# Shared-expert weight tiles lent to the routed-expert stream; shared gate loaded and multiplied later

## The reference, cut to what matters

```python
def moe_ffn(h, router_w, router_bias, w_gate, w_up, w_down, ws_gate, ws_up, ws_down):
    t = h.reshape(-1, d)
    scores = jax.nn.sigmoid((t @ router_w).astype(jnp.float32))
    ...
    _, top_idx = lax.top_k(jnp.where(exp_mask, biased, -jnp.inf), TOP_K)
    ...
    def expert_block(args):
        tb, gb = args
        a = jax.nn.silu(jnp.einsum('td,edf->tef', tb, w_gate)) * jnp.einsum('td,edf->tef', tb, w_up)
        return jnp.einsum('tef,efd->td', a * gb[..., None], w_down)
    ...
    shared = (jax.nn.silu(t @ ws_gate) * (t @ ws_up)) @ ws_down
```

## Time and profile before

| | |
|---|---|
| median of 3 runs | 642.48 us (641.2 to 643.05) |
| the profiled execution | 643.33 us, of which the span is 641.7 us |
| PE busy | 581.4 us, 91% of the span |
| DMA traffic | 252.55 MB, mean 394 GB/s |
| mean granted PE clock | 0.974 of full |
| chain that ended last | PE 70%, DMA 20%, SP's queue 4% |

### The profile page before, as it was taken

How to read it: one execution, slowest core, us unless ns; L and a number is a source line. 1 busy time by engine, 2 the same in 40 slices (tenths; PEclk the granted TensorE clock), 3 DMA queues, 4 the chain that set the end, 5 groups by cost and what they waited for, 6 DMA issues and landing times.

```text
span 641.7 us, 11143 instructions
## 1 busy us (share of the span) xinstructions
PE 581.4 (91%) x4568; PEld 404.7 (63%) x4568; DVE 211.7 (33%) x479; ACT 167.6 (26%) x308; POOL 32.7 (5%) x78
## 2 busy tenths in 40 slices
PE   0789999999999999989999999596999999998776
PEld 0478777688867576756675757363667676765343
DVE  0287777787832222011212221020121212122104
ACT  3164726672622121111221212010212121212010
POOL 1240210010200000000000000000000000000002
PEclk9989999999999999999999999797999999999779
DMA  8999599989998999999999999999999999999995
GB/s 330 386 332 400 205 367 379 411 314 398 420 388 367 393 422 416 421 422 419 421 421 421 420 421 421 421 421 421 420 421 421 419 422 422 420 420 421 422 386 172
DMA packets 50662, 252.55 MB, mean 394 GB/s; under 512 B 5912, under 2 KB 11680, under 8 KB 26288
## 3 DMA queue, kind: packets, MB, share of 16 engines
q1 hardware_dynamic: 47808, 245.85, 94.5%
q0 software_dynamic: 1840, 4.21, 2.1%
q10 hardware_dynamic: 960, 1.74, 0.7%
HBM read 250.06 MB, written 1.72 MB: 392 GB/s over the span
## 4 chain that ended last, share of the span: by engine, by line
PE 70%; DMA 20%; SPq 4%; ACT 2%; DVE 2%; issue 1%; POOL 0%; POOLq 0%; DVEq 0%; ACTq 0%
PE bank L1286 24%; PE bank L1361 12%; DMA ring<-in_w_up 8%; PE bank L1257 7%; PE bank L1303 7%; DMA ring<-in_w_gate 4%; DMA ring<-in_w_in 4%; SPq L572 3%; PE bank L856 2%; DMA ring<-in_w_mod 2%; PE bank L898 2%; PE bank L906 2%; PE bank L902 2%; DMA ccol<-in_c 2%; PE bank L1019 1%; PE bank L1220 1%
## 5 line engine op out<-in xcount | busy, mean ns | idle before, releaser
L1286 PE MATMUL bank<-ring,xe 128*64 128x256 f32 (+1 forms) x1520 | 176.6, 401 | 10.5 <-DMA ring<-in_w_up 8.7
L1286 PEld LDWEIGHTS bank<-ring,xe 128*64 128x64 f32 (+1 forms) x1520 | 111.0, 132 | 50.4 <-issue 24.8
L1361 PE MATMUL bank<-ring,actT 128*64 128x512 f32 (+1 forms) x384 | 86.6, 627 | 6.8 <-DMA ring<-in_w_down 5.2
L2334 DVE TENSOR_TENSOR act_e<-bank,sil 128x256 f32<-128x256 f32 x26 | 11.0, 424 | 187.9 <-ACT sil L1749 187.9
L2348 DVE SCALAR_TENSOR_TENSOR ylo<-bank,gslot,yhi 128x512 fp32r<-128x512 f32 x50 | 37.5, 751 | 83.9 <-ACT yhi L1762 83.9
L1762 ACT ACTIVATE yhi<-bank,gslot 128x512 fp32r<-128x512 f32 x50 | 34.4, 687 | 116.5 <-PE bank L1361 116.5
L1749 ACT ACTIVATE sil<-bank 128x256 f32<-128x256 f32 x26 | 10.0, 385 | 192.1 <-PE bank L1286 192.1
L1257 PE MATMUL bank<-pone,hhi 128*128 128x256 f32 x200 | 50.0, 288 | 0.0
L1361 PEld LDWEIGHTS bank<-ring,actT 128*64 128x64 f32 (+1 forms) x384 | 25.4, 132 | 37.7 <-issue 37.4
L1257 PE MATMUL bank<-pone,hlo 128*128 128x256 f32 x200 | 48.9, 282 | 0.0
L1286 PE MATMUL bank<-rows_tile,xe 128*64 128x256 f32 (+1 forms) x128 | 34.2, 428 | 9.8 <-DMA ring<-in_w_up 6.3
(11 more groups left out here) (388 smaller groups left out, 838.9 us busy)
## 6 DMA issues: line engine op xcount, KB each, us to landing
ring<-in_w_gate SPq DMA_DIRECT2D x49, 1024.0 KB, 25.0
ring<-in_w_down SPq DMA_DIRECT2D x48, 1024.0 KB, 26.3
ring<-in_w_up SPq DMA_DIRECT2D x46, 1024.0 KB, 26.1
ring<-in_w_mod SPq DMA_DIRECT2D x12, 2048.0 KB, 13.9
ring<-in_w_in SPq DMA_DIRECT2D x5, 2048.0 KB, 16.5
gb<-in_w_up SPq DMA_DIRECT2D x5, 1024.0 KB, 23.8
spare<-in_w_gate SPq DMA_DIRECT2D x4, 1024.0 KB, 26.8
ring<-in_w_out SPq DMA_DIRECT2D x2, 2048.0 KB, 18.8
```

The costliest lines, as they stand in the source:

```text
L1286: ins = mm(bank[6][j * w:(j + 1) * w, part * FE:(part + 1) * FE], xe[:, k, slots], weights[:, k, :], start=(k == 0), stop=(k == KD - 1))
L1361: ins = mm(bank[4 + h][j * w:(j + 1) * w, :], actT[:, f, j * w:(j + 1) * w], weights[:, f, 512 * h:512 * h + 512], start=(f == 0), stop=(f ...
```

## The change

The three tiles of `ws` become three more places of the stream (`WS_UP`, `WS_DOWN`, `WS_GATE`). The first fill grows from 16 tiles to 19: g = 18, 16 and 17 are loaded where, and when, the shared gate, up and down were. `rows_tile` takes g = 22 instead of g = 20: it used to follow four refills and now follows three.

The shared gate is loaded just ahead of g = 37, into `WS_GATE`, once g = 18 has been used (in unit 1), and stays. `WS_UP` and `WS_DOWN` go on serving the stream up to unit 8; shared up and down are loaded ahead of g = 107, the last tile of unit 8, once g = 89 and g = 90 have been used.

PE multiplies no shared gate before the counts; it multiplies both halves in unit 2, and ACT applies one Silu to 512 columns instead of two to 256. The bank that held the first half is no longer waited for. The semaphores of the three products are one, and PE waits for each tile's load.

```diff
-SPARE, OVER_GB, OVER_XN, OVER_Y, OVER_ROWS = NTILE, NTILE + 1, NTILE + 2, NTILE + 3, NTILE + 4
-FILL = [0, 1, OVER_Y, 2, 3, 4, 5, 6, 7, 8, 9, 10, OVER_XN, SPARE, OVER_GB, 11]
-ROWS_FREE = len(FILL) + 4
+SPARE, OVER_GB, OVER_XN, OVER_Y, OVER_ROWS, WS_UP, WS_DOWN, WS_GATE = range(NTILE, NTILE + 8)
+FILL = [0, 1, OVER_Y, 2, 3, 4, 5, 6, 7, 8, 9, 10, OVER_XN, SPARE, OVER_GB, 11, WS_UP, WS_DOWN, WS_GATE]
+ROWS_FREE = len(FILL) + 3
+SHARED_UNIT = 8
...
-        while place[taken] == OVER_Y or (kept == OVER_GB and place[taken] in (OVER_GB, OVER_XN)):
+        while (place[taken] == OVER_Y or (kept == OVER_GB and place[taken] in (OVER_GB, OVER_XN)) or
+               place[taken] == WS_GATE or (len(place) >= SHARED_UNIT * NTILE and place[taken] in (WS_UP, WS_DOWN))):
+            if place[taken] in (WS_UP, WS_DOWN, WS_GATE):
+                shared[place[taken]] = (len(place), taken)
             taken += 1
...
-            sp.dma_start(ws[:, 0:EW].rearrange("p (k f) -> p k f", k=KD),
-                         t["ws_gate"][0].rearrange("(k p) f -> p k f", k=KD)).then_inc(wsg_loaded, 16)
-            sp.dma_start(ws[:, EW:2 * EW].rearrange("p (k f) -> p k f", k=KD),
-                         t["ws_up"][0].rearrange("(k p) f -> p k f", k=KD)).then_inc(ws_loaded, 16)
+            load_first(NTILE + 6)
+            load_first(NTILE + 4)
...
-            sp.dma_start(ws[:, 2 * EW:3 * EW], t["ws_down"][0].rearrange("(p j) n -> p (j n)", j=JF)).then_inc(ws_loaded, 16)
+            load_first(NTILE + 5)
...
+            def load_shared(at):
+                for where_, (g, taken) in SHARED.items():
+                    if g == at:
+                        released(taken)
+                        if where_ in (WS_UP, WS_GATE):
+                            source = t["ws_up" if where_ == WS_UP else "ws_gate"][0]
+                            sp.dma_start(tile(where_).rearrange("p (k f) -> p k f", k=KD),
+                                         source.rearrange("(k p) f -> p k f", k=KD)).then_inc(tile_loaded[where_], 16)
+                        else:
+                            sp.dma_start(tile(WS_DOWN),
+                                         t["ws_down"][0].rearrange("(p j) n -> p (j n)", j=JF)).then_inc(tile_loaded[WS_DOWN], 16)
...
                     g = unit * NTILE + i
+                    load_shared(g)
...
-            pe.wait_ge(wsg_loaded, 16)
-            complete("sg0", shared_product(claim("sg0"), 0, (0,)))
...
-                shared_product(bank[7], 0, (1,)).then_inc(sg_filled, 1)
+                pe.wait_ge(tile_loaded[WS_GATE], PLACE.count(WS_GATE) * 16 + 16)
+                shared_product(bank[7], 0).then_inc(shared_filled, 1)
...
-            ps = product(act, "sg0")
-            drain("sg0", A(ssil[:, 0, :], ps[:, 0:NST * P], ACT.Silu))
...
-                A(ssil[:, 1, :], bank[7][:, NST * P:2 * NST * P], ACT.Silu).then_inc(sg_copied, 1)
+                A(ssil[:, :, :], bank[7][:, :].rearrange("p (a b) -> p a b", a=JF), ACT.Silu).then_inc(sg_copied, 1)
```

More of the change, by code:

```diff
@@ L66 @@
 FIRST_STEP = [sum(1 if v in QUAD_UNITS else 2 for v in range(u)) for u in range(UNITS)]
-SPARE, OVER_GB, OVER_XN, OVER_Y, OVER_ROWS = NTILE, NTILE + 1, NTILE + 2, NTILE + 3, NTILE + 4
-FILL = [0, 1, OVER_Y, 2, 3, 4, 5, 6, 7, 8, 9, 10, OVER_XN, SPARE, OVER_GB, 11]
-ROWS_FREE = len(FILL) + 4
+SPARE, OVER_GB, OVER_XN, OVER_Y, OVER_ROWS, WS_UP, WS_DOWN, WS_GATE = range(NTILE, NTILE + 8)
+FILL = [0, 1, OVER_Y, 2, 3, 4, 5, 6, 7, 8, 9, 10, OVER_XN, SPARE, OVER_GB, 11, WS_UP, WS_DOWN, WS_GATE]
+ROWS_FREE = len(FILL) + 3
+SHARED_UNIT = 8
 def place_tiles():
-    place, replaces, free = list(FILL), [None] * len(FILL), []
+    place, replaces, shared = list(FILL), [None] * len(FILL), {}
     taken = 0
@@ L87, in place_tiles @@
     nth = [place[:g + 1].count(p) for g, p in enumerate(place)]
-    return place, replaces, nth
-PLACE, REPLACES, NTH = place_tiles()
+    return place, replaces, nth, shared
+PLACE, REPLACES, NTH, SHARED = place_tiles()
 def build(nc, t, o, overflow_at=CAP):
@@ L125, in build @@
         plan += [("hb0_0", 7, 2), ("hb0_1", 3, 2)] + banks("x2T1:2 x2T3:0 rt1:5") + [("hb1_0", 2, 2), ("hb1_1", 6, 2)]
-        plan += banks("sg0:4 pos:1 counts:5")
+        plan += banks("pos:1 counts:5")
         plan = [(name, b, 2 if name in ("pv0", "pv1", "hm0", "hm1", "xT0", "xT1", "xT2", "xT3") else reads)
@@ L332, in build @@
         qk_loaded, grow_loaded, ml_loaded, cm_loaded = sem("qk_loaded"), sem("grow_loaded"), sem("ml_loaded"), sem("cm_loaded")
-        wsg_loaded, ws_loaded, rt_loaded = sem("wsg_loaded"), sem("ws_loaded"), sem("rt_loaded")
+        rt_loaded = sem("rt_loaded")
         consts, const_masks = sem("consts"), sem("const_masks")
@@ L365, in build @@
         hT_low, hT_high = sem("hT_low"), sem("hT_high")
-        sg_filled, sg_copied = sem("sg_filled"), sem("sg_copied")
+        shared_filled, sg_copied = sem("shared_filled"), sem("sg_copied")
         dve_done, pool_done = sem("dve_done"), sem("pool_done")
         out_done = sem("out_done")
-        tile_loaded = [sem(f"tile_loaded{i}") for i in range(NTILE + 5)]
+        tile_loaded = [sem(f"tile_loaded{i}") for i in range(NTILE + 8)]
         last_columns = [sem(f"last_columns{i}") for i in range(2)]
@@ L380, in build @@
         y_filled, y_hi, y_lo = sem("y_filled"), sem("y_hi"), sem("y_lo")
-        gate_ready, su_filled = sem("gate_ready"), sem("su_filled")
+        gate_ready = sem("gate_ready")
         c_used, all_done, scaled, last_gated = sem("c_used"), sem("all_done"), sem("scaled"), sem("last_gated")
@@ L479, in tile @@
             if i >= NTILE:
-                return (spare[:, :], gb[:, :, :].rearrange("p s d -> p (s d)"), xn[:, 0:EW], over_yhl[:, :], rows_tile[:, :])[i - NTILE]
+                return (spare[:, :], gb[:, :, :].rearrange("p s d -> p (s d)"), xn[:, 0:EW], over_yhl[:, :], rows_tile[:, :],
+                        ws[:, EW:2 * EW], ws[:, 2 * EW:3 * EW], ws[:, 0:EW])[i - NTILE]
             return ring[:, i * EW:(i + 1) * EW]
@@ L1169, in _, with shared_product @@
             turn_back(1)
-            def shared_product(ps, off, parts=range(JF)):
+            def shared_product(ps, off):
                 w = ws[:, off:off + EW].rearrange("p (k f) -> p k f", k=KD)
-                for j in parts:
+                for j in range(JF):
                     for k in range(KD):
@@ L1210, in shared_up @@
             def shared_up():
-                pe.wait_ge(ws_loaded, 32)
-                shared_product(bank[7], EW).then_inc(su_filled, 1)
+                pe.wait_ge(tile_loaded[WS_UP], PLACE.count(WS_UP) * 16 + 16)
+                shared_product(bank[7], EW).then_inc(shared_filled, 1)
             def shared_down():
+                pe.wait_ge(tile_loaded[WS_DOWN], PLACE.count(WS_DOWN) * 16 + 16)
                 wd = ws[:, 2 * EW:].rearrange("p (j n) -> p j n", j=JF)
@@ L1230, in gather_first @@
                 evacuated(pe, "x2T3")
-                evacuated(pe, "sg0")
+                evacuated(pe, "rt0")
                 pe.wait_ge(first_stream, 1)
@@ L1764, in shared_gate @@
             def shared_gate():
-                act.wait_ge(sg_filled, 1)
-                A(ssil[:, 1, :], bank[7][:, NST * P:2 * NST * P], ACT.Silu).then_inc(sg_copied, 1)
+                act.wait_ge(shared_filled, 1)
+                A(ssil[:, :, :], bank[7][:, :].rearrange("p (a b) -> p a b", a=JF), ACT.Silu).then_inc(sg_copied, 1)
             def keep_g2(n, first):
@@ L2391, in shared_act @@
             def shared_act():
-                dve.wait_ge(su_filled, 1)
+                dve.wait_ge(shared_filled, 2)
                 dve.wait_ge(sg_copied, 1)
```

## The result

| | before | changed |
|---|---|---|
| median | 641.79 us (640.78 to 643.05, 6 runs) | 645.32 us (644.59 to 646.97, 6 runs) |
| ratio | | 1.0056, 95% interval 1.0043 to 1.0069 |
| profiled execution | 643.33 us, span 641.7 us | 644.59 us, span 643.0 us |
| mean granted PE clock | 0.974 | 0.963 |

The change made the kernel 3.5 us slower, 0.56%. The forecast was 3.3 us: 645.8 against a median of 642.48. The two profiled executions lie only 1.3 us apart, because the one of the changed kernel was 1.7 us ahead when the routing was done (171.89 us against 173.58). It was 0.7 us ahead at 17 us, in code that the change doesn't touch.

What follows compares the result with a forecast made beforehand. DMA traffic was taken to bound the kernel from 216 us on. Against the profiled 643.33 us, 0 (memory) + 0 (rows tile) + 0.9 (1 KB pieces) + 0 (shared gate) + 2.4 (clock) = 646.6; as median 645.8 us, range 643.0 to 647.2.

Steps and rivals of the forecast that it cites:

- The bound: From 216 us on, DMA traffic at 421 GB/s sets the end; only earlier bytes or a faster rest would help.
- The lent memory at 0: Three routed tiles replace three shared ones in the first fill, adding no bytes by 216 us: 0.
- The rows tile at 0: Loading `rows_tile` earlier gains up to 2.1 us at 192 to 196 us, lost again after 212 us: 0.
- the second hole: Traffic dip to 199 GB/s from 192 to 196 us, costing 2.1 us; forecast to be filled by `rows_tile`.
- the third: Traffic dip to 320 GB/s from 212 to 216 us, costing 1.0 us; forecast to grow by 2.1 us.
- The 1 KB pieces at 0.9 us: Shared gate and up, loaded in the full stretch at 356 GB/s instead of 421, cost 2 x 0.46 us.
- The clock at 2.4 us: PE idle 3.85 us before the counts; its clock halves, delaying the first gate product and whole stream by 2.4 us.
- the open gap: PE's idle time from 169.73 to 173.58 us, before the counts, where the eight matmuls were taken out: 3.85 us.
- No fall: Rival: PE's clock stays at 1.00 after the gap, leaving only 0.9 us: 643.4 us, same by measurement; chance 0.21.

Runs made afterwards that it cites:

- e6_not_lent: Changed kernel with the first fill cut to the old 16 tiles and the `ws` memory empty until the late shared loads: 652.22 us, ratio 1.0145 to the kernel before.
- e9_delay: Kernel before plus eight dense matmuls, result unused, directly ahead of the first gate product: 646.03 us against 641.76, ratio 1.0056.
- e1_fill: Changed kernel with eight matmuls, result unused, put back on PE ahead of the counts: 643.38 us against 642.53 for the kernel before, ratio 1.0013.
- e2_fill_8k: e1_fill with shared gate and up also read as 8 KB rows per partition: 642.49 us, ratio 0.9992 to the kernel before.
- e3_gate_moved: Kernel before with only the shared gate's first half moved from before the counts to unit 2: 644.23 us against 642.53, ratio 1.0028.
- e8_gap_fill: Kernel before plus two matmuls, result unused, between the counts and the gather: 641.66 us against 641.76, ratio 0.9996.
- e10_fill_both: Changed kernel with eight matmuls ahead of the counts and two between counts and gather: 643.06 us against 642.28 for the kernel before, ratio 1.0021.
- e4_rows_early: Kernel before with only `rows_tile` moved to follow three refills instead of four: 642.21 us against 642.53, ratio 0.9995.

## Why the prediction was right

- **The bound.** Right. From 216 us to the end of the stream the traffic is full in both kernels, PE's longer work in unit 2 disappeared in its waits, and `e6_not_lent` and `e9_delay` priced the two things that count before: a place (1.9 to 2.3 us) and PE's time ahead of the first release (about 1 us for 1 us, with an interval of 2.2 to 4.9 us for 3.4).
- **The lent memory at 0.** Right. `e6_not_lent` shows that the value is large but was there before.
- **The rows tile at 0.** Right in its effect, in part wrong in its working. The forecast had the second hole vanish and the third grow by 2.1 us; in the kernel with that edit alone the second shrank by 0.7 us and the third grew by 0.1. The sum took for granted that the few tiles issued there keep the engines at 421; the 381 GB/s say that they didn't, and why stays open. In the changed kernel the second hole kept 1.7 us and the third grew by 0.3. There `rows_tile` came free later than forecast, too: its cast starts at 190.83, 18.9 us after the first count instead of 16.4 (189.98 - 173.58), as much later as PE's first gate product.
- **The 1 KB pieces at 0.9 us.** Right in place and, as far as times can tell, in size: 0.9 us by the medians between `e1_fill` and `e2_fill_8k`. That it is the size of the pieces, and not how far apart they lie, is not shown. The Trainium skill (DMA: Bandwidth & Descriptors, Specifications) has transfers from 512 B on at line rate. These loads in pieces of 1 KB ran below it, at 350 against 423 GB/s.
- **The clock at 2.4 us.** Right. The fall came 4.0 us after PE stopped (168.04 to 172.03), inside the 2.4 to 4.2 us read from the rows, and lasted the 6.8 us read from them; PE lost 2.54 us. Such closeness is partly luck: in the four profiles with the open gap the fall came 2.0 to 4.5 us after PE stopped and lasted 6.8 or 10.2 us. Over many executions the cost is 1.8 us with the gate moved, 1.8 to 2.6 with only the pieces mended, 2.8 between the changed kernel and its filled form. Where it is smaller than PE's 2.54 us, the kernel before may lose something itself in some executions; no run shows that. That the emptied place on PE costs the time is shown by `e3_gate_moved` and `e1_fill`. That it does so through the clock is read from the profiles: each kernel with a larger interval had the fall, none without it did, and in the fall the same gather matmuls took longer (1.05 us instead of 0.64). The clock itself can't be set.
- **No fall**, the rival on the other side, did not happen in any of the four profiles with the open gap.

Not foreseen: that filling the gap would leave a fall of 3.4 us, in both profiled executions. The forecast took the clock of the kernel before as always full at this place.

## What to carry to other kernels

Work that fills a wait is not free to move: before shifting it to where an engine "has room", ask what the emptied place does to PE's clock, and whether anything is paced by PE just behind it. Memory lent to a stream pays only if it stood empty when the stream ran dry; count the bytes that can have landed by the last dry moment, in both versions, before counting on a deeper ring. And a load with small pieces that hides in a dry phase should not be moved into a saturated one.

## What the runs showed of the hardware that was not expected

- PE's clock fell though the first gap was filled: in `e1_fill`, `e2_fill_8k` and `e9_delay` at 174 to 175 us, for 3.4 us, with no idle stretch longer than 0.72 us there, only seven small matmuls in about 1 us between two short gaps. With the second gap filled as well (`e8_gap_fill`, `e10_fill_both`), neither of two profiles had it; but two profiles with it open, the kernel before and `e4_rows_early`, hadn't either. Whether the fall is excluded by the filling or only rarer, they can't tell.
- A fall doesn't need a gap of 3.49 us, the shortest that the forecast had seen with one. In the changed kernel's own trace PE waited 2.80 and 2.06 us for tiles, and 0.8 and 1.0 us after the work had come the clock fell, for 3.4 us each time:

```profile
594.50 0.41 PE L1303 MATMUL bank<-ring,xe 128*32 128x256 f32 x2 [2.80 <-DMA ring<-in_w_up]
604.55 5.34 PE L1378 MATMUL bank<-ring,actT 128*32 128x512 f32 x32 [2.06 <-DMA ring<-in_w_down]
```

```profile
595.50:596.00 0.50, 0.50 (x12) 0.34 (x8) 0.00 (x0) 0.00 (x0) 0.00 (x0) 0.50 0.94 393
605.50:606.00 0.50, 0.50 (x8) 0.06 (x4) 0.00 (x0) 0.00 (x0) 0.00 (x0) 0.52 0.90 377
```

- Around the routing, the length of the low stretches was 3.4, 6.8 or 10.2 us, though the dense work began at the same place in the code. The longest came in one of the four kernels with the open gap: the same idle time costs 2.5 us in one execution and 3.2 in another.
- Reads in pieces of 1 KB, 128 KB apart, moved at 356 GB/s before and pulled a 3 us stretch of the changed kernel down to 381 (350 in `e1_fill`), where rows of 8 KB keep 421 to 426.
